# Compression layer of a two-block transformer kernel: the first matmuls with the weights stationary and the gathered token blocks moving

## The reference

```python
def compress_tokens(t, tok_idx, pos, w1, w2):
    blocks = t[:, :, tok_idx] + pos.astype(t.dtype)
    flat = blocks.reshape(blocks.shape[0], blocks.shape[1], blocks.shape[2], -1)
    return jax.nn.silu(flat @ w1) @ w2
```

## Time and profile before

| what | value |
|---|---|
| median of three runs | 1100.22 us |
| lowest, highest run | 1091.24, 1101.83 us |
| span of the profiled execution | 1093.0 us |
| its own time | not listed apart from the span |
| granted TensorE clock, mean over the span | 0.957 |
| PE, DVE, ACT, POOL busy | 91%, 73%, 21%, 38% |
| HBM read, mean rate | 158.33 MB, 146 GB/s |

### The profile page before, as it was taken

The page is one execution under the profiler, slowest core; times in us unless marked ns, Lnnn a source line. Parts: engine busy times, 40 slices in busy tenths (PEclk is TensorE's granted clock), DMA queues, the critical chain, the costliest instruction groups (busy, mean ns, idle before and its releaser), DMA issues.

```text
span 1093.0 us, 13616 instructions
## 1 busy us (share of the span) xinstructions
PE 998.1 (91%) x5129; PEld 829.4 (76%) x5129; DVE 799.2 (73%) x813; ACT 231.3 (21%) x544; POOL 416.6 (38%) x289
## 2 busy tenths in 40 slices
PE   5997989999998979397999999889899989999996
PEld 5885678888887868277888888667666768888885
DVE  5869479767676899857967776699577358677674
ACT  2114221011112149132110111100223321111111
POOL 5431035444433898213444444353300023333331
PEclk9998999999998999689999999999869999999998
DMA  8751416554662440032564654362403015655640
GB/s 301 251 195 59 135 35 219 185 215 157 227 221 92 160 144 1 0 116 95 178 228 154 211 211 158 127 210 87 173 1 114 2 39 193 197 188 191 192 154 38
DMA packets 81043, 159.95 MB, mean 146 GB/s; under 512 B 4893, under 2 KB 40681, under 8 KB 81002
## 3 DMA queue, kind: packets, MB, share of 16 engines
q1 hardware_dynamic: 80714, 158.80, 42.5%
q10 hardware_dynamic: 288, 0.59, 0.1%
HBM read 158.33 MB, written 1.05 MB: 146 GB/s over the span
## 4 chain that ended last, share of the span: by engine, by line
PE 65%; DVE 26%; POOL 3%; ACT 3%; issue 2%; DMA 1%; POOLq 0%; SPq 0%; DVEq 0%; ACTq 0%
PE ps L1591 62%; DVE w_lo L635 7%; DVE arena L934 6%; PE ps L1595 3%; POOL w_hi L498 2%; DVE nrm L703 2%; DVE x_res L695 1%; DVE arena L747 1%; ACT arena L1276 1%; DMA raw<-in_even_w_in 1%; DVE act_hl L712 1%; ACT act_hl L1298 1%; DVE arena L959 1%; POOL st L541 1%; DVE nrm L744 0%
## 5 line engine op out<-in xcount | busy, mean ns | idle before, releaser
L1591 PE MATMUL ps<-act_hl,w_hi 128*128 128x512 f32 (+1 forms) x1248 | 379.1, 379 | 15.0 <-DVE act_hl L712 9.5
L635 DVE TENSOR_TENSOR w_lo<-raw,w_hi 128x2048 fp32r<-128x2048 f32 (+3 forms) x133 | 326.6, 2482 | 47.5 <-POOL w_hi L498 23.4
L1591 PE MATMUL ps<-act_hl,w_lo 128*128 128x256 f32 x1088 | 281.1, 282 | 0.0
L1591 PEld LDWEIGHTS ps<-act_hl,w_hi 128*128 128x128 f32 x1248 | 222.1, 199 | 61.3 <-DVE act_hl L712 13.8
L498 POOL TENSOR_SCALAR w_hi<-raw 128x2048 fp32r<-128x2048 f32 (+5 forms) x62 | 135.4, 2186 | 210.8 <-PE ps L1591 191.5
L513 POOL TENSOR_SCALAR w_hi<-raw 128x2048 fp32r<-128x2048 f32 x56 | 136.9, 2446 | 180.2 <-PE ps L1591 180.2
L1591 PE MATMUL ps<-w_hi,hl 128*128 128x512 f32 (+1 forms) x712 | 191.1, 382 | 6.0 <-DVE w_lo L635 6.0
L1591 PEld LDWEIGHTS ps<-act_hl,w_lo 128*128 128x128 f32 x1088 | 195.4, 190 | 0.8
L1591 PE MATMUL ps<-w_hi,act_hl 128*128 128x512 f32 (+2 forms) x528 | 142.5, 387 | 10.5 <-DVE arena L1024 3.9
L1591 PEld LDWEIGHTS ps<-w_hi,hl 128*128 128x128 f32 (+1 forms) x712 | 126.9, 182 | 32.8 <-issue 5.8
L1591 PEld LDWEIGHTS ps<-w_hi,act_hl 128*128 128x128 f32 x528 | 96.2, 192 | 33.0 <-DVE arena L1024 4.2
(11 more groups left out here) (184 smaller groups left out, 841.7 us busy)
## 6 DMA issues: line engine op xcount, KB each, us to landing
raw<-in_mlp_w SPq DMA_DIRECT2D x64, 1024.0 KB, 5.2
raw<-in_w_gate SPq DMA_DIRECT2D x22, 512.0 KB, 4.0
raw<-in_w_up SPq DMA_DIRECT2D x22, 512.0 KB, 4.9
raw<-in_w_down SPq DMA_DIRECT2D x11, 1024.0 KB, 4.9
raw<-in_odd_w_pw SPq DMA_DIRECT2D x16, 512.0 KB, 4.9
raw<-in_w_in SPq DMA_DIRECT2D x8, 1024.0 KB, 5.0
raw<-in_even_w_in SPq DMA_DIRECT2D x6, 1024.0 KB, 8.5
raw<-in_even_w_out SPq DMA_DIRECT2D x4, 1024.0 KB, 6.3
```

The lines of the kernel that those rows point to most:

```text
L635: tt(w_lo[slot_of(n)][:, 0:w], raw[slot_of(n)][:, 0:w], w_hi[slot_of(n)][:, 0:w].bitcast(F32), ALU.subtract).then_inc(S("w_split"), 1)
L1591: return pe.matmul(o, l, r, start=start, stop=stop, skip_group_check=True)
```

## The change

The compression's first layer takes 128x128 blocks of the weights as stationary operand and the columns of `f2` as moving one. For each contraction block and each half `c` of the 256 inner units there are two matmuls: `w_hi` with all 60 columns (high and low side by side) and `w_lo` with the 30 high ones. The result is [128 inner units] x [60] for each half, and its two parts of 30 columns have to be added. ACT copies the low part to SBUF, DVE adds it to the high part, ACT takes the tanh, and DVE writes `hidc` and `hidrep` with (tanh + 1) times x. The four transposes and the wait of PE on `hid` are gone, and the memset of `hidrep` is issued ahead of the waits.

```diff
-        hce = nrm[0:30, 1, 0:512].rearrange("p (a n) -> p a n", a=2)
-        hid = nrm[0:30, 1, 512:1024].rearrange("p (a n) -> p a n", a=2)
+        hlo, hid, hce = (nrm[:, 1, at:at + 120].rearrange("p (a c n) -> p a c n", a=2, c=2) for at in (512, 640, 768))
...
+        def cmp_out(a_):
+
+            return ps[:, ACC + 2 * a_:ACC + 2 * a_ + 2, 0:64]
...
+                link(dve.memset(hidrep, 0.0))
                 for a_ in range(2):
-                    dve.wait_ge(S("hc_tanh"), a_ + 1)
-                    stt(hid[:, a_, :], hce[:, a_, :], 1.0, ps[0:30, ACC + 2 * a_, 0:256], ALU.add, ALU.mult)\
-                        .then_inc(S("hid"), 1)
-
-                link(dve.memset(hidrep, 0.0))
-                dve.wait_ge(S("hid_turned"), 1)
-                hT = ps[:, ACC + 3, 0:120].rearrange("p (a c n) -> p a c n", a=2, c=2)
-                dve.tensor_copy(hidc, hT[:, 0])
+                    dve.wait_ge(S("hid_low"), a_ + 1)
+                    tt(hid[:, a_], cmp_out(a_)[:, :, 0:30], hlo[:, a_], ALU.add).then_inc(S("hid"), 1)
+                dve.wait_ge(S("hid"), 2)
+                dve.wait_ge(S("hc_tanh"), 1)
+                stt(hidc, hce[:, 0], 1.0, hid[:, 0], ALU.add, ALU.mult)
+                dve.wait_ge(S("hc_tanh"), 2)
                 for c in range(2):
-                    ins = dve.tensor_copy(
-                        hidrep[:, c].rearrange("p (g r) n -> p g r n", g=2)[:, :, :, 0:15],
-                        hT[:, 1, c, :].rearrange("p (g n) -> p g n", g=2).unsqueeze(2).to_broadcast([P, 2, 4, 15]))
+                    for g in range(2):
+                        tanh, pre = (v[:, 1, c, 15 * g:15 * g + 15].unsqueeze(1).to_broadcast([P, 4, 15]) for v in (hce, hid))
+                        ins = stt(hidrep[:, c, 4 * g:4 * g + 4, 0:15], tanh, 1.0, pre, ALU.add, ALU.mult)
                 ins.then_inc(S("hidc"), 1)
...
                     piece_done(FIRST["cmp"] + 2 * a_ + 1)
-                    f(hce[:, a_, :], ps[0:30, ACC + 2 * a_, 0:256], ACT.Tanh, scale=0.5).then_inc(S("hc_tanh"), 1)
+                    f(hlo[:, a_], cmp_out(a_)[:, :, 30:60], ACT.Copy).then_inc(S("hid_low"), 1)
+                    act.wait_ge(S("hid"), a_ + 1)
+                    f(hce[:, a_], hid[:, a_], ACT.Tanh, scale=0.5).then_inc(S("hc_tanh"), 1)
...
                         for kk in range(8):
-                            high, low = (f2[:, 16 * a_ + 8 * h + kk, 30 * i:30 * i + 30] for i in range(2))
-                            for i, (lt, w) in enumerate(((high, w_hi), (high, w_lo), (low, w_hi))):
-                                ins = mm(ps[0:30, ACC + 2 * a_, 0:256], lt, piece_of(w, n)[:, kk, :],
-                                         h == 0 and kk == 0 and i == 0, h == 1 and kk == 7 and i == 2)
+                            k = 16 * a_ + 8 * h + kk
+                            for c in range(2):
+                                s = slice(c * P, (c + 1) * P)
+                                mm(cmp_out(a_)[:, c, 0:60], piece_of(w_hi, n)[:, kk, s], f2[:, k, :],
+                                   h == 0 and kk == 0, False)
+                                ins = mm(cmp_out(a_)[:, c, 0:30], piece_of(w_lo, n)[:, kk, s], f2[:, k, 0:30],
+                                         False, h == 1 and kk == 7)
                         ins.then_inc(S("pe_piece"), 1)
...
-                pe.wait_ge(S("hid"), 2)
-                for a_ in range(2):
-                    for c in range(2):
-                        at = 60 * a_ + 30 * c
-                        ins = turn(ps[:, ACC + 3, at:at + 30], hid[:, a_, c * P:(c + 1) * P])
-                ins.then_inc(S("hid_turned"), 1)
```

## The result

The changed kernel took 1106.58 us in the median of 8 runs (1104.79 to 1110.74), the kernel before 1099.45 in 8 (1091.24 to 1102.66). The ratio is 1.0082, with a 95% interval of [1.0058, 1.0106]: 9.0 us slower, 6 to 12. The medians alone differ by 7.1. All runs of this document are compared as they came, but for one execution of 2433.43 us in run 4, which its ratio leaves out. The profiled execution of the changed kernel took 1107.5 us at a span of 1105.6, so some 2 us lie around a span.

What follows compares the result with a forecast made beforehand. PE was taken to bound the kernel from 774.31 us on, DVE's splits before that. Pieces +6.6, transposes +1.6 + 0.4 - 0.4 made +8.2 us, carried to the median 1100.22: 1108.4 us, range 1097 to 1117.

Steps and rivals of the forecast that it cites:

- Pace of the matmuls: Compression on PE: loads set the pace, 0.115 us a matmul at full clock and 0.213 at half.
- The clock: Compression on PE: thin columns let the clock fall 2.6 us after the start, and nothing in its four pieces raises it.
- The pieces: Compression's four pieces: the last ends at 789.0 in place of 782.4, +6.6 us.
- The cover: PE's waits inside the compression: 3.5 us of idle before 774.3 is used up, all that can hide a longer compression.
- Transposes: Behind the compression: 16 at half clock +1.6 us, half of the next 8 +0.4, four gone -0.4.
- Tail on ACT and DVE: Work behind the last piece: zero, as slower transposes cover it; +0.2 us on ACT if the clock is full.
- Attention: Attention behind the compression: its own 17 us at half clock stay as they are.
- A: Start of the attention: the clock stays low into it, +6.8 us more, 1115.2 us; chance 0.25.
- B: Compression: the loads hold full clock, every matmul at 0.115 us, -0.8 us, 1099.4 us; chance 0.12.
- C: Attention: the later half-clock stretch of 17 us shortens, +1.8 us in all, 1102.0 us; chance 0.08.
- D: Compression: full 128-column loads are faster than partial ones, 0.06 us a matmul, 1097.6 us; chance 0.05.

Runs made afterwards that it cites:

- run 4: Changed kernel without its 64 compression matmuls on w_lo, so without their products: 1101.37 us, ratio 1.0034 to the kernel before.
- run 1: Changed kernel with 256 moving columns in all 128 compression matmuls in place of 60 or 30: 1100.43 us, ratio 1.002 to the kernel before.
- run 2: Changed kernel with 128 moving columns in all 128 compression matmuls in place of 60 or 30: 1106.9 us, ratio 1.0076 to the kernel before.
- run 7: Changed kernel with the compressed attention's small products widened (128 columns for 30, 64 for 15): 1108.07 us, ratio 1.007 to the kernel before.
- run 8: Changed kernel with 256 moving columns in the compression and the attention's small products widened: 1094.29 us, ratio 0.9972 to the kernel before.
- second profile: Both kernels profiled once more with no edit: changed kernel 1103.95 us, kernel before 1097.08 us.
- run 6: Kernel before with the compressed attention's small products widened (128 columns for 30, 64 for 15): 1093.51 us, ratio 0.9959 to the kernel before.

## Why the prediction was right

The forecast was 1108.4 us with a shift of +8.2; measured are 1106.58 and +9.0 (+6 to +12), or +7.1 in the medians. The shift is clear of the noise, and under the 1% (11 us) that the prediction took as what can be told from no change. By its steps:

- *Pace of the matmuls.* 0.115 us forecast at full clock, (764.35 - 763.47) / 8 = 0.110 measured. 0.213 forecast at half clock; measured (789.67 - 764.92) / 116 = 0.213, from the 13th matmul to the first transpose. The two rows that carried it, four fp32 loads with 30 columns and the 160-column matmuls, were good neighbours.
- *The clock.* It fell 1.2 us after the first thin matmul in one profile and 2.5 in the other, where I took 2.6 (2.3 to 3.0 from two cases). Where I had 22.6 matmuls at full clock, some 12 ran before the starts spread (764.92), so some 11 more cost 0.1 us extra each, 1.0 us. Runs 1 and 2, and 7 and 8, show that the columns decide here: same loads, same count, other columns.
- *The pieces.* +6.6 forecast. The transposes begin at 789.83 against 782.57, +7.3. Forecast were 25.0 us from 764.0, measured are 26.4 from 763.5: the earlier fall makes it longer, the earlier start takes part of it back.
- *The cover.* Forecast: 3.5 us of idle before the third piece is used up, and cmp 1 to 3 don't wait. The chain has 128 matmuls without a break. The 0.87 us of wait ahead of cmp 1 are used up as well.
- *Transposes.* +1.6 forecast with the four that go; 5.22 against 3.13 measured, +2.1. All 24 ran at half clock, not 20 of them.
- *Tail on ACT and DVE.* Zero forecast. DVE's last small product ends at 792.5 and the first scores start at 795.0, as soon as the transposes are through. With thick columns (run 1) they come 2.8 us behind the compression, and ACT and DVE stand in the chain then (1.95 us of copies behind 0.7 of the new tail). PE waits 0.17 us for them there, as against the +0.2 given for a full clock. So the zero holds behind slow transposes, and the tail is small otherwise.
- *Attention.* Forecast as before. The first pair of profiles has +9.4 us at the first scores and +12.6 at the end, the second +8.0 and +6.9. The difference between the pairs is the length of the half-clock stretch there. Over all executions it doesn't look like the change's doing: by the estimate from the mean clocks the changed kernel has 24 us more at half clock than before, and its compression with the transposes alone accounts for 24 (30.7 against 6.8, first profiles) to 27 (27.3 against none, second ones). An open end stays: counted from the compression's start, the first scores come 9.9 and 11.7 us later than before, and the time is only 7 to 9 us longer. The start itself lies anywhere from 763.5 to 773.0 in the 13 profiles, by what runs ahead of it, so differences of absolute times between two profiles say little below that.

The rivals. *A* (clock low into the attention) is wrong in its mechanism: full clock came back at 795.4, 0.4 us behind the first scores, and at 796.9, 0.4 us before them, in the second profile. What had run at half clock ahead of that were the thin matmuls, over some 25 us without bringing it back, then 5 us of transposes (and in the first profile 0.4 us of scores). In the run with 128 columns it was back at 797.1, within the transposes. The Trainium skill's rule in "TensorE: Matmul & The Clock Gate", Part 4 (PE-mode transpose), by which transposes don't bring full clock, is contradicted by these rows as by the earlier trace rows. A longer half-clock stretch later on would look like A; the estimate from the mean clocks leaves no room for one on average, though run 7, with 33 us more at half clock than run 6 where its compression and transposes account for 31, leaves a little. *B* (the loads hold the clock) is wrong: PEld was busy for the whole compression while the clock was at half. *C*: the stretch in the attention didn't go, but its length does vary, 10.2 to 27.3 us in nine profiles. *D*: behind loads of 128 columns the starts were 0.11 us apart at full clock, no faster than the 0.113 of the earlier trace rows.

What was right by luck: I gave the attention no change from a single profile, and runs show it to vary by 17 us of half clock. The total is also closer than its parts: counted from the compression's start the part ahead of the scores was 9.9 to 11.7 us, over the forecast 8.2.

## What to carry to other kernels

In this kernel a matmul cost what was longer, its load or its columns, and both went with the clock: a load of 128 columns 0.11 us at full and 0.21 at half, 256 moving columns behind a small load 0.12 and 0.21. Turning the operands so that few columns move behind full loads saved columns that the loads then cost again, and lost the clock for all of it. So look in the trace for the nearest stretch with as few columns behind each load, and read the granted clock there. Where the load sets the pace, moving more columns than needed can be free, and can pay: 4.5 us in the attention of the kernel before, 6 us in the compression of the changed one, 13.8 between runs 7 and 8. It needs a measurement each time: 128 columns in the compression (run 2) and the attention's widening alone in the changed kernel (run 7) brought nothing.

## What the runs showed that was not expected

- 128 moving columns at a load of 128 didn't hold the clock in the profile, although PE was busy in all records; 256 did. In the attention 64 in place of 15 columns in the fp32 products on 64 rows, and 128 for 30 in the four behind full loads, held it together.
- PE's program in the kernel before has a reserve that the page doesn't show: inside the compression it waits for splits for 3.2 to 4.4 us (four profiles with 96 matmuls of 256 columns), which a longer compression could use. The changed kernel has none left.
- A matmul of 60 columns behind a 30-column load takes 0.03 us at full clock (24 in 0.8 us), behind a 128-column load 0.11.
